# Second block of each last mixing projection by seven half products, with half of the MLP norm put off into it

## The reference

```python
merged = jax.nn.sigmoid(ga) * y_conv + jax.nn.sigmoid(gb) * y_ret
x = x + merged @ w_o                      # w_o: 1024 x 1024, the last mixing projection
h2 = rmsnorm(x, norm_mlp)
return x + jnp.square(jax.nn.relu(h2 @ w_up)) @ w_down     # w_up: 1024 x 4096
```

## Time and profile before

| | |
|---|---|
| time, median of 3 runs | 2099.52 us (2098.48 to 2100.42) |
| profiled execution, first to last instruction | 2097.1 us |
| PE busy | 2074.6 us, 99% |
| PEld busy | 1869.8 us, 89% |
| DVE busy | 1564.8 us, 75% |
| ACT busy | 1067.8 us, 51% |
| matmuls | 12382 |
| chain that ended last | PE 83%, DVE 3%, ACT 1%, issue 1% |

### The profile page before, as it was taken

How to read it: one execution, slowest core, us unless ns; L and a number is a source line. 1 busy time by engine, 2 the same in 40 slices (tenths; PEclk the granted TensorE clock), 3 DMA queues, 4 the chain that set the end, 5 groups by cost and what they waited for, 6 DMA issues and landing times.

```text
span 2097.1 us, 30779 instructions
## 1 busy us (share of the span) xinstructions
PE 2074.6 (99%) x12382; PEld 1869.8 (89%) x12382; DVE 1564.8 (75%) x2113; ACT 1067.8 (51%) x1522; POOL 27.3 (1%) x36
## 2 busy tenths in 40 slices
PE   9999999999999999999999999999999999999998
PEld 8888878878888899988999998888899988999997
DVE  8787785768656778866878887756778866868884
ACT  5776474646434445524555654434445534555653
POOL 0000000000000000000000000000000000000000
PEclk9999999999999999999999999999999999999999
DMA  5332222212322234432434353322234432344352
GB/s 186 111 101 100 91 81 71 91 66 84 107 85 87 81 111 136 146 111 91 121 107 118 118 162 105 107 91 81 91 101 141 145 107 91 121 115 118 114 175 83
DMA packets 63870, 227.96 MB, mean 109 GB/s; under 512 B 7216, under 2 KB 7600, under 8 KB 63600
## 3 DMA queue, kind: packets, MB, share of 16 engines
q1 hardware_dynamic: 59040, 208.83, 29.8%
q0 software_dynamic: 4544, 17.04, 4.7%
q10 hardware_dynamic: 144, 0.12, 0.0%
HBM read 223.86 MB, written 2.10 MB: 108 GB/s over the span
## 4 chain that ended last, share of the span: by engine, by line
PE 83%; DVE 3%; ACT 1%; issue 1%; DVEq 0%; ACTq 0%
PE bank L846 15%; PE bank L848 15%; PE bank L847 15%; PE bank L891 9%; PE bank L895 9%; PE bank L893 9%; PE bank L841 2%; PE bank L842 2%; PE bank L843 2%; PE bank L1100 1%; PE bank L1092 1%; ACT arena L1676 0%; PE bank L1169 0%; PE bank L1170 0%; PE bank L1168 0%
## 5 line engine op out<-in xcount | busy, mean ns | idle before, releaser
L1894 DVE TENSOR_TENSOR w_lo<-w_raw,w_hi 128x1024 fp32r<-128x1024 f32 x477 | 572.3, 1216 | 370.9 <-ACT w_hi L1271 368.9
L1271 ACT ACTIVATE w_hi<-w_raw 128x1024 fp32r<-128x1024 f32 x477 | 490.9, 1047 | 513.8 <-PE bank L848 333.1
L846 PE MATMUL bank<-h_both,w_hi 128*128 128x512 f32 x956 | 365.2, 382 | 2.0 <-DVE arena L1940 1.1
L847 PE MATMUL bank<-h_both,w_hi 128*128 128x512 f32 x956 | 362.3, 379 | 0.0
L848 PE MATMUL bank<-h_both,w_lo 128*128 128x512 f32 x956 | 362.3, 379 | 0.0
L846 PE MATMUL bank<-y_hi,w_hi 128*128 128x512 f32 x920 | 351.1, 382 | 5.4 <-DVE y_lo L1945 3.4
L848 PE MATMUL bank<-y_hi,w_lo 128*128 128x512 f32 x920 | 349.4, 380 | 0.0
L847 PE MATMUL bank<-y_lo,w_hi 128*128 128x512 f32 x920 | 349.2, 380 | 0.0
L846 PEld LDWEIGHTS bank<-h_both,w_hi 128*128 128x128 f32 x956 | 180.7, 189 | 30.1 <-issue 3.5
L847 PEld LDWEIGHTS bank<-h_both,w_hi 128*128 128x128 f32 x956 | 180.7, 189 | 25.9 <-issue 1.0
L848 PEld LDWEIGHTS bank<-h_both,w_lo 128*128 128x128 f32 x956 | 180.7, 189 | 25.6
(11 more groups left out here) (340 smaller groups left out, 3624.9 us busy)
## 6 DMA issues: line engine op xcount, KB each, us to landing
w_raw<-in_stream SPq DMA_DIRECT2D x389, 512.0 KB, 3.6
w_raw<-in_stream POOLq DMA_DIRECT2D x30, 512.0 KB, 5.4
x<-in_x_t SPq DMA_DIRECT2D x8, 256.0 KB, 6.7
out_t<-x SPq DMA_DIRECT2D x8, 256.0 KB, 2.1
arena<-in_consts POOLq DMA_DIRECT2D x1, 1024.0 KB, 5.2
w_raw<-in_stream SPq DMA_DIRECT2D x2, 256.0 KB, 4.3
arena<-in_positions POOLq DMA_DIRECT2D x1, 256.0 KB, 6.0
vec_t<-in_vecs ACTq DMA_DIRECT2D x1, 112.5 KB, 3.2
```

The costliest lines, as they stand in the source:

```text
L846: pe.matmul(out, w_hi[:, slot, w], streamed(a_h), start=first, stop=False)
L847: pe.matmul(out, w_hi[:, slot, w], streamed(a_l), start=False, stop=False)
L1271: A.activation(w_hi[:, slot, w], w_raw[:, chunks.raw_slot[raw], w], ACT.Copy).then_inc(hi_ready, 1)
L1894: V.tensor_tensor(w_lo[:, slot, w], src[:, w], w_hi[:, slot, w].bitcast(F32), ALU.subtract).then_inc(lo_ready, 1)
```

## The change

O1 is done by seven half products. Its mixed inputs are made by DVE and ACT inside O0, from the merged tiles in `ga_t` (four sums of 128 x 1024, where the down turns have three left to do at that place). Part 0 of the norm is no longer emitted behind O0: its two halves go into `owed` and are paid inside O1, on ACT both behind the first bank copy, on DVE one behind B21's remainder and one behind T3's. Part 1 stays behind O1, but its first square waits for the last of the four tiles (`whole`), since O1 finishes them together. `mix` no longer prepares the next operand (`behind`), since O1 does. The weights of O1 are stored in quarters.

```diff
+    def merged_product():
+        first, second = s("norm", gain="mlp", part=0, owing=True), s("norm", gain="mlp", part=1, whole=True)
+        return [s("residual", 4, 1, k="m", j=0, ymix=True), first, s("residual", 0, 1, k="m", j=1, seven=True), second]
...
-        return [s("mix"), s("up", 4, 1, j=0, led=True, owing=True), s("up", 0, 1, j=1, seven=True, mixing=True)]
+        return [s("mix", behind=True), s("up", 4, 1, j=0, led=True, owing=True), s("up", 0, 1, j=1, seven=True, mixing=True)]
...
@@ ACT, y_highs @@
-                    act.wait_ge(summed, T.value("sums", 3))
+                    act.wait_ge(summed, T.value("sums", step.incs["sums"]))
...
-                for i, (n, slot) in enumerate(split_slots(T, step)):
-                    high(i)
-                    if i == 2:
+                for n, slot in split_slots(T, step):
+                    if n < RING:
+                        act.wait_ge(bank_ready, T.value("turn", 0, 4))
+                        round_ahead(n, slot)
+                        continue
+                    high(n - RING)
+                    if n - RING == 2:
                         high(3)
                     act.wait_ge(chunk_used, T.value("used", n - RING + 1))
                     round_ahead(n, slot)
...
@@ ACT, norm @@
-                        added(i)
+                        added(DT // 2 - 1 if step.args.get("whole") else i)
                         square(DT // 2 + i, i)
...
+            def owe_norm(step):
+                read, sums = T.value("turn", -4, 4), T.value("vec")
+                gains = [gain_column(step, k) for k in range(DT // 2)]
+                def two(first):
+                    for k in (first, first + 1):
+                        act.wait_ge(evacuated, read + k + 1)
+                        A.activation(h_hi[:, k, :], x[:, k, :], ACT.Copy, scale=gains[k]).then_inc(a_hi, 1)
+                        if k >= 2:
+                            act.wait_ge(vec, sums + k - 1)
+                        A.activation(xsq[:, k % 2, :], x[:, k, :], ACT.Square).then_inc(act_out, 1)
+                owed.extend((lambda: two(0), lambda: two(2)))
...
@@ DVE, y_mix @@
+                if len(ahead) > AHEAD:
+                    remainder(*ahead.pop(0))
+                if step.args["k"] == "m":
+                    dve.wait_ge(vec, T.value("vec"))
+                    V.tensor_tensor(y_sum(step, 0), m_late(0), m_late(1), ALU.add).then_inc(summed, 1)
+                    V.tensor_tensor(y_sum(step, 2), m_early(0), m_late(0), ALU.subtract).then_inc(summed, 1)
+                    dve.wait_ge(summed, sums + 1)
+                    V.tensor_tensor(y_sum(step, 1), m_early(0), y_sum(step, 0), ALU.subtract).then_inc(summed, 1)
+                    dve.wait_ge(summed, sums + 3)
+                    V.tensor_tensor(y_sum(step, 3), m_early(1), y_sum(step, 1), ALU.add).then_inc(summed, 1)
...
@@ DVE, seven @@
-                    if kind == "up":
+                    if kind == "up" or step.args.get("k") == "m":
                         pay(1)
                     ahead(4)
+                    if step.args.get("k") == "m":
+                        pay(1)
```

More of the change, by code:

```diff
@@ L207, in s @@
         if args.get("ymix"):
-            more = {"sums": 1, "act_out": 1} if kind == "up" else {"sums": 3, "mixes": 4}
+            more = {"sums": 1, "act_out": 1} if kind == "up" else {"sums": 4 if args["k"] == "m" else 3, "mixes": 4}
             incs = {**incs, **{k: incs.get(k, 0) + v for k, v in more.items()}}
@@ L541, in mixed_part @@
             if step.kind == "residual":
-                return y_part(part, n)
+                return y_part(step, part, n)
             if not in_rest(step):
@@ L599, in kept @@
         def kept(T, step, n):
-            if step.kind == "ga" and T.var("half") == 1:
+            if (step.kind == "ga" and T.var("half") == 1) or step.args.get("k") == "m":
                 return tmp2[:, n, :]
@@ L1246, in runs_ahead @@
         def runs_ahead(step):
-            return step.args.get("beside") or step.args.get("ahead") or step.kind == "mix"
+            return step.args.get("beside") or step.args.get("ahead") or (step.kind == "mix" and not step.args.get("behind"))
         def next_slot(T):
@@ L1356, in seven @@
                         act.wait_ge(vec, T.value("vec", -4))
-                    if step.kind in ("up", "residual"):
+                    if step.kind == "up" or step.args.get("k") == "y":
                         act.wait_ge(vec, T.value("vec"))
@@ L2089, in norm, with owe_norm, two @@
                     add_square(k, i + 1, i)
+            def owe_norm(step):
+                highs, squares_made, sums = T.value("a_hi"), T.value("act_out"), T.value("vec")
+                gains = [gain_column(step, k) for k in range(DT // 2)]
+                def two(first):
+                    for k in (first, first + 1):
+                        dve.wait_ge(a_hi, highs + k + 1)
+                        V.scalar_tensor_tensor(out=h_lo[:, k, :], in0=x[:, k, :], scalar=gains[k],
+                                               in1=h_hi[:, k, :].bitcast(F32), op0=ALU.mult,
+                                               op1=ALU.subtract).then_inc(a_lo, 1)
+                        dve.wait_ge(act_out, squares_made + k + 1)
+                        if k == 0:
+                            V.tensor_copy(sumsq[:, :], xsq[:, 0, :]).then_inc(vec, 1)
+                        else:
+                            dve.wait_ge(vec, sums + k)
+                            V.tensor_tensor(sumsq[:, :], sumsq[:, :], xsq[:, k % 2, :], ALU.add).then_inc(vec, 1)
+                owed.extend((lambda: two(0), lambda: two(2)))
             def x_step(step):
@@ L2159, in residual, with sums_of_y @@
                     V.tensor_tensor(x_n, product_bank(n), x_n, ALU.add).then_inc(evacuated, 1)
+            def sums_of_y(step, late, sums):
+                dve.wait_ge(act_out, T.value("act_out"))
+                dve.wait_ge(a_lo, T.value("a_lo"))
+                dve.wait_ge(summed, sums)
+                V.tensor_tensor(y_sum(step, 0), y_sum(step, 0), late, ALU.add).then_inc(summed, 1)
+                V.tensor_tensor(y_sum(step, 1), y_sum(step, 2), late, ALU.subtract).then_inc(summed, 1)
+                dve.wait_ge(summed, sums + 2)
+                V.tensor_tensor(y_sum(step, 3), y_sum(step, 3), y_sum(step, 1), ALU.add).then_inc(summed, 1)
+                dve.wait_ge(summed, sums + 3)
             def y_mix(step):
@@ L2890, in order_of_weights @@
         elif kind == "residual" and args["k"] == "m":
-            out.append(group(w_o[layer], [(512 * j, 512)]))
+            of_block = w_o[layer][:, 512 * j:512 * j + 512]
+            out.append(quarters(of_block) if args.get("seven") else group(w_o[layer], [(512 * j, 512)]))
         elif kind == "residual":
```

44 lines of the change are left out of this document (28 added, 16 removed).

## The result

The changed kernel takes 2114.24 us (median of 4 runs, 2113.76 to 2115.11), beside 2099.65 us (4 runs, 2098.48 to 2100.42) of the kernel before: 1.007 times as long (95% interval 1.0056 to 1.0085), 14.6 us more. The forecast was 7.6 us more, 2107.1 us; the direction was right, the size was not, and the time lies above the range.

What follows compares the result with a forecast made beforehand. PE's own pace was taken as the bound, with DVE lacking room here. Per layer +3.8 us, for two +7.6: 2097.1 becomes 2104.7, plus 2.4 gives 2107.1 us; own range 2105.7 to 2108.5, full range 2102.3 to 2110.3.

Steps and rivals of the forecast that it cites:

- The spacings of matmuls: On PE: 216 ns in plain turns, 112 ns by half products, so O1 without waits would save 1.95 us a layer.
- O0's additions: Layer 0, on DVE: the additions onto `x` start at 967.5 instead of 961.1, behind four new sums.
- O1's three waits: PE in O1: waits of 0.4, 2.4 and 0.85 us for B21, T3 and B22; O1 ends 2.0 us later.
- The chain to U1: From O1's last additions through the norm: first mixed sum for U1 goes from 991.35 to 997.0, everything 5.6 us late.
- How much of this PE feels is read at U1's fifth product ... The slack is 1.8 us.: U1's fifth product: 5.6 us of lateness less 1.8 of slack makes it start 3.8 us later, per layer.
- This number doesn't depend on the waits inside O1.: The 3.8 us a layer stays whatever O1 waits; of it O1 shows 2.0 and U1 1.8.
- Rival C, the clock: Clock falls to half rate behind O1's 2.4 us wait: +0.5 to +1.7 us a layer, 2108.1 to 2110.5 us; 9%.
- falls in U1 too: Case of the clock rival: a fall in U1 as well shows all 1.7 us of lost matmul work a layer.
- Rivals A and B: A: saving stays, T3 in time in O1, 2095.6 us, 5%. B: only O1 waits, +2.0 a layer, 2103.5 us, 14%.
- The sum's last step: From profiled execution to median of the runs: 2.4 us added to 2104.7, giving 2107.1 us.

Runs made afterwards that it cites:

- e1: Changed kernel with U1's first bank copy moved on ACT ahead of U0's four relus and B21's rounding: 2106.96 us.
- e2: Changed kernel with the put-off half norm not paid ahead of T3 in O1 but in the later places: 2114.8 us.
- e6: Changed kernel with the edits of e1 and e2 together: 2109.32 us.
- e4: Changed kernel with 40 small matmuls on PE ahead of U1's third product, which makes U1's output wrong: 2110.89 us.
- e5: Kernel before, not the changed one, with the same copy move as e1: 2099.33 us beside 2098.9 us, ratio 1.0002.
- e8: Changed kernel with the MLP norm's part 0 not put off but done at once behind O0's additions: 2122.41 us, ratio 1.0112.
- e9: Changed kernel plus e1's edit, put-off norm's second half behind T3's rounding on ACT, both halves behind T3's remainder on DVE: 2108.15 us.
- e3: Changed kernel with the MLP norm's squares and sums on 8 of 512 columns, leaving out this norm's sum of squares: 2104.47 us.

## Why the prediction was right and wrong

- **The spacings of matmuls** are said to be those of columns / 2.4 + 2.5 ns. That gives 216 ns for 512 columns but 109 for 256, where the trace has 112. The sum uses the trace's and doesn't suffer.
- **O0's additions** forecast at 967.5. Right: 968.07 in a trace whose O1 starts 0.6 us later (963.37 against 962.77).
- **O1's three waits** forecast 0.4, 2.4 and 0.85 us, all told, at the fourth, fifth and sixth product. Measured, idle time: 0.16, 2.19 and 0.72, and with the pick-up O1 is 1.90 us longer (forecast 2.0). Right.
- **The chain to U1** forecast 5.6 us late at the first mixed sum. Measured 5.8: 997.74 - 963.37 = 34.37 us behind O1's start against 991.35 - 962.77 = 28.58. Right. The rows of DVE after:

```profile
989.55 0.68 DVE L2801 TENSOR_TENSOR x<-bank,x 128x512 f32<-128x512 f32 x1
991.21 3.08 DVE L2108 TENSOR_TENSOR sumsq<-sumsq,arena 128x512 f32<-128x512 f32 x4 [0.97 <-ACT arena L1598]
994.21 2.73 DVE L2097 SCALAR_TENSOR_TENSOR h_both<-x,vec_t,h_both 128x512 fp32r<-128x512 f32 x4
997.74 0.48 DVE L2702 SCALAR_TENSOR_TENSOR arena<-x,vec_t,arena 128x256 f32<-128x256 f32 x1 [0.80 <-ACT arena L1463]
```

- **"How much of this PE feels is read at U1's fifth product ... The slack is 1.8 us."** This is the step that failed. The slack has to be the smallest over all seven products, and the third has 0.27 us, through the first bank copy and what stands ahead of it on ACT. With it the sum would have been 5.8 - 0.27 = 5.5 us a layer, 11.0 for two, 2110.6 us (2110.2 with the forecast's own 5.6). The prediction even says that "the products ahead of it wait for part of that", and didn't ask which one for how much. e1 shows it: with the copy moved, the changed kernel takes 2106.96 us.
- **"This number doesn't depend on the waits inside O1."** Right as far as tested: e2 and e6 take T3's wait out and the time doesn't fall.
- **Rival C, the clock.** It was looked for behind T3's wait in O1 (2.19 us, clock stays at 1.00 in both layers). It fell behind the wait that wasn't foreseen, twice 1.7 us; e4, where it doesn't fall there, is 3.0 to 3.35 us shorter. 11.0 + 3.4 = 14.4 us, the result within 0.2. The case "falls in U1 too" stood in the text with +1.7 a layer, on top of too small a wait.
- **Rivals A and B** are out: O1 and U1 both wait.
- **The sum's last step** holds: the median (2114.24) lies 1.4 us above the traced span (2112.8), where 2.4 were counted; no part of the miss.

## What to carry to other kernels

When a chain gets later by a known amount, don't read the slack at the product that looks last; list for each product what it waits for, with the queue that stands ahead of that releaser, and take the smallest. An instruction that is ready early but queued behind late ones inherits their lateness, and putting it first can cost nothing (e5) and be worth half the loss (e1). And where VectorE is full for a whole turn, as here, work taken from TensorE was no gain while VectorE's own chain stayed as long: moving the norm's half about (e2, e6, e8) moved the wait with it or made it longer.

## What the runs showed of the hardware

TensorE's granted clock fell to 0.50, that is 1.2 GHz, behind waits much shorter than the 3.4 us of the earlier trace rows. Per wait, with its idle time: after U1's 2.94 and 2.93 us in the changed kernel it fell in both layers; behind e8's 2.93 us in both; behind e9's 2.73 and 2.74 us in both; behind e3's 2.21 us in layer 1, and not behind its 1.52 in layer 0. Behind O1's 2.19 us it stayed at 1.00 in both layers of the changed kernel, but in e1 it fell behind the same wait in layer 1 (2.19 us) and not in layer 0 (2.18 us), and so it did in e4. The rows of e1:

```profile
975.51:978.90 3.39, 2.94 (x24) 2.75 (x24) 3.39 (x5) 2.93 (x4) 0.00 (x0) 1.00 0.49 160
1764.42:1767.81 3.39, 3.39 (x21) 3.39 (x22) 3.39 (x5) 2.52 (x3) 0.00 (x0) 0.68 0.45 160
```

And e2 has 2.94 us in both layers, with a fall behind the first (0.50) and none behind the second:

```profile
1015.49:1018.00 2.51, 2.51 (x12) 2.51 (x13) 2.00 (x3) 2.51 (x4) 0.00 (x0) 0.50 1.02 201
...
1808.38:1811.00 2.62, 2.62 (x23) 2.62 (x24) 2.11 (x3) 2.62 (x4) 0.00 (x0) 1.00 1.00 189
```

Even the 3.4 us of the earlier trace rows, from which the prediction took its case of a fall, come without one in e3, whose same wait is 3.40 us long:

```profile
161.63:165.04 3.41, 3.40 (x16) 3.01 (x17) 1.67 (x3) 3.38 (x6) 0.00 (x0) 1.00 0.49 159
```

So in these runs waits of 2.2, 2.9 and 3.4 us each came with a fall and without one, and the length alone doesn't tell. A forecast over such a wait should hold both cases. What a fall costs depends on what follows: in U1 1.7 us in full, in e1's O1 0.65 us (23.24 against 22.59 us), since the next product would have waited anyway. The Trainium skill, TensorE: Matmul & The Clock Gate, What's actually happening, says that an idle TensorE goes back to 1.2 GHz; the trace agrees for U1's wait in the changed kernel, and e4, with that wait mostly filled, has no fall there. It doesn't agree for e2's wait of 2.94 us in layer 1 and e3's of 3.40 us, behind which the clock stays at 1.00.
